# Second scale and shift on transposed columns, modulation units summed in groups, and a new order from the first norm to the first expert

## The chip, the cores and the metric

The kernel runs on one core of a Trainium2 chip. The metric is the device time in microseconds (us) of one launch; a smaller time is better. The engines are PE (TensorE), DVE (VectorE), ACT (ScalarE), POOL (GpSimd) and SP (SyncE, which here only issues DMAs). Each takes its own instructions in the order of the program; semaphores order them against each other.

## What is computed

One layer on 384 tokens (128 context tokens and 256 latent ones), three tiles of 128 tokens, D = 1024 features. The reference, cut to what matters:

```
sh1, sc1, g1, sh2, sc2, g2 = silu(cond) @ w_ada + b_ada      # for two conditions: context, latent
h  = x * (1 + sc1) + sh1
u  = h @ w_in                                                # 1536 columns
mix = concat(rglru(conv(u_r)) * gelu(u_g), fourier(u_f)) @ w_out
x  = layer_norm(ALPHA * x + g1 * mix, ln1_g, ln1_b)
h2 = x * (1 + sc2) + sh2
y2 = hier_moe(h2)      # logits; best of 4 groups; best 2 of its 4 experts; 16 SwiGLU experts
x  = layer_norm(ALPHA * x + g2 * y2, ln2_g, ln2_b)
```

## The kernel before

Weights stream through a ring of SBUF slots, one unit of 2 MB (1024 x 512 floats) a slot. The first 17 units (`p1_units`) are twelve of w_ada, three of w_in and two of w_out; six slots hold them. Then come 48 units of the experts (gate, up, down of 16 experts), with a seventh slot. SP issues each load when its slot is free: it waits for `p1_used` in the first part and for `unit_used` in the experts, both of which PE raises when it has consumed a unit. The seventh slot lies over `rows` and is free when POOL has finished the first norm (`x1_done`).

**Modulation.** For each w_ada unit, `ada_sums` runs 8 matmuls of 32 x 512 into a PSUM bank (two of the 32 rows are in use, one a condition), ACT copies the bank to `mrow` (`ada_rows`), PE turns it into columns of `modT` by 4 tiny matmuls (`ada_cols`), and DVE adds the bias (`mod_out`). In the middle of the kernel these units (4 to 9) stand in a row between the Fourier work and the output projection.

**Output projection, norm, h2.** PE computes `mix` for tile 0, 1, 2 in two halves of 512 columns each (L1447, 8 matmuls a half; what the text calls the mix). Between the quarters it makes six rows by L1431 (g1, 1+sc2 and sh2, for both conditions, each copied to all partitions), which ACT copies to SBUF. DVE multiplies by the g1 row, adds ALPHA * x, takes the statistics, and applies scale and shift in token-major form with the sc2 and sh2 rows (`tts`). PE transposes `tts` (L1460), ACT copies it to `h2T`, and PE computes the router logits (L1466). ACT rounds `tts` to `h2H`, DVE takes the rest `h2L`; the pair feeds the dispatch.

**Routing.** DVE picks group and experts from the logits with a chain of small operations (L927 to L965), PE turns the marks into ranks (L1490, L1495; called rank below), DVE builds the selection matrices `sel` (`pick` L984, `pick2` L994, six of each), the counts `cnt` (`route_done`), `io` and the weights `comb`. The **dispatch** (L1509) multiplies h2H and h2L by `sel`: 16 blocks n, 6 matmuls each, in the four PSUM banks 4 to 7; from n = 4 on it waits until ACT has copied block n-4 out (`x_out`, L577). ACT then copies the columns of one expert to `xs` (`x_in`), and PE starts the first expert (L1553).

**Experts.** `project_in(e, 0)`, `project_in(e, 1)`, `turn`, `project_out`, `combine` for e = 0 to 15, software pipelined; then the second norm on DVE.

The order on every engine is written by hand. In the text, start of the picks means the first L984.

Of the kernel before, what the change touches and what calls it, by code (L numbers as in the profile page):

```python
# [15 lines left out]
P = 128  # L16
D = 1024
# [41 lines left out]
C_ROW = C_SUM + 2  # L59
# [17 lines left out]
def constants():  # L77
# [10 lines left out]
    for q in range(2):  # L88
        c[q::32, C_SUM + q] = 1
# [24 lines left out]
def build(nc, t):  # L114

    ctx = ExitStack()
    with ctx:
# [15 lines left out]
        def keep(name, shape, dt=F32):  # L133
# [13 lines left out]
        cond32 = keep("cond32", [P, KD, 32])  # L147
# [24 lines left out]
        tts3 = at("tts3", A0 + 6144, [P, NT, D])  # L172
        tts = [tts3[:, i, :] for i in range(NT)]
# [48 lines left out]
        rows = at("rows", rows0, [P, 8, D])  # L222
# [22 lines left out]
            "x1_done h2_done mod2_done h2hi h2lo h2T_ps h2T_sb lg_ps assign_done rank_ps route_done "  # L245
# [47 lines left out]
        ADA_GROUPS = [2, 4, 6, 10, 12]  # L293
        ADA_UNIT = [0, 1, 3, 4, 7, 8, 9, 10, 11, 12, 15, 16]
        ADA_COUNT = [1, 2, 3, 4, 8, 9, 10, 11, 12, 13, 16, 17]

        ABANK = [6, 6, 4, 6] + [6, 4] * 3 + [6, 6]
# [4 lines left out]
        ]  # L302

# [54 lines left out]
        def _(sp):  # L358
# [54 lines left out]
        def _(act):  # L413
# [28 lines left out]
            def ada_rows(n):  # L442

                act.wait_ge(s["p1_used"], ADA_COUNT[n])
                need(act, "modT_ps", n)
                act.copy(mrow[:, :], PS[:, ABANK[n], :]).then_inc(s["mrow_sb"], 1)  # L446

# [82 lines left out]
            for n in range(4, 10):  # L530
                ada_rows(n)


            act.wait_ge(s["yr_done"], CR)
            for r in range(6):
                act.wait_ge(s["row_ps"], r + 1)
                act.copy(rows[:, r, :], PS[:, 6:8, :].rearrange("p a n -> p (a n)")).then_inc(s["row_sb"], 1)
                if r == 1:
                    root(NT)
                if r == 0:  # L540
                    for k, n in enumerate(("ln1_g", "ln1_b")):
                        act.dma_start(rows[:, 6 + k, :], t[n].partition_broadcast(P)).then_inc(s["ln1_in"], 16)


            def h2_copies(i):
                act.wait_ge(s["h2T_ps"], i + 1)
                act.copy(h2T[:, :, i * P:(i + 1) * P], PS[:, 2 * i:2 * i + 2, :].rearrange("p a (k n) -> p (a k) n", n=P))\
                    .then_inc(s["h2T_sb"], 1)

            def h2_high(i):  # L550
                act.wait_ge(s["h2_done"], i + 1)
                if i == 0:
                    act.wait_ge(s["p1_used"], 15)
                act.copy(h2H[:, i, :], tts[i]).then_inc(s["h2hi"], 1)

            root(NT + 1)
            ada_rows(10)
            h2_high(0)
            h2_copies(0)
            root(NT + 2)  # L560
            ada_rows(11)
            h2_high(1)
            h2_copies(1)
            h2_copies(2)
            h2_high(2)

            act.wait_ge(s["assign_done"], 1)
# [11 lines left out]
            act.wait_ge(s["route_done"], 1)  # L579
            for n in range(KD):  # L580
                if n == 0:
                    act.wait_ge(s["h2lo"], NT)
                    act.wait_ge(s["lg_ps"], 1)
                x_out(n)
            act.wait_ge(s["prow_ps"], 1)
            act.copy(Prow[:, :, :], PS[:, 2:4, 0:TOK]).then_inc(s["prow_sb"], 1)
            for n in range(KD, 2 * KD):
                x_out(n)


            counts = {}

            def x_in(e):
# [4 lines left out]
                if e == 0:  # L598
# [3 lines left out]
                if e >= 2:  # L602
                    used(act, unit(e - 2, 1))
# [44 lines left out]
            x_in(0)  # L648
# [46 lines left out]
        def _(dve):  # L695
# [41 lines left out]
            dve.tensor_copy(cond32[:, :, 0:2], cond[:, :, :]).then_inc(s["cond_done"], 1)  # L737
# [29 lines left out]
            def mod_out(n):  # L767

                c0 = ADA[n][0] * KD + 4 * ADA[n][1]

                dve.wait_ge(s["modT_ps"], next(g for g in ADA_GROUPS if g > n))
                dve.tensor_tensor(modT[:, c0:c0 + 4, :], PS[:, 7, 2 * c0:2 * c0 + 8].rearrange("p (n s) -> p n s", s=2),
                                  cols[:, A_BADA + c0:A_BADA + c0 + 4].unsqueeze(2).broadcast_to([P, 4, 2]),
                                  ALU.add).then_inc(s["mod_sb"], 1)

            def modulate(hf):

                mod_out(2 * hf)
                mod_out(2 * hf + 1)
                dve.wait_ge(s["mod_sb"], 2 * hf + 2)  # L780
# [89 lines left out]
            for n in range(4, 10):  # L870
                mod_out(n)
            dve.wait_ge(s["mod_sb"], 10)


            sc2 = modT[:, SC2 * KD:SC2 * KD + KD, :]
            sh2 = modT[:, SH2 * KD:SH2 * KD + KD, :]
            g1col = cols[:, A_L1G:A_L1G + KD].unsqueeze(2).broadcast_to([P, KD, 2])
# [857 lines left out]
```

## Time and profile before

| | |
|---|---|
| device time, 3 runs | 543.44 us median (543.39 to 551.8) |
| the profiled execution | 546.24 us |
| its span, first to last instruction | 544.4 us |
| PE, DVE, ACT, POOL busy | 465.0, 244.5, 120.6, 61.4 us |
| mean granted clock of PE | 0.936 |
| moved by DMA | 146.64 MB |

The profiled execution took 546.24 us, of which 544.4 are between its first and its last instruction. Positions below are us from the start of this span. A granted clock of 1.00 is 2.4 GHz, one of 0.50 is 1.2 GHz; a value between is a stretch in which both occurred. An fp32 matmul stands in the trace as two records, so the 8 matmuls of `ada_sums` are "x16" and 8 transposes may be "x8" or more.

### The profile page before, as it was taken

What the parts mean: (1) busy time and instruction counts of PE and PEld (TensorE: products, weight loads), DVE (VectorE), ACT (ScalarE), POOL (GpSimd) and SP (SyncE); (2) the same over time, 40 slices, a digit from 0 to 9 for tenths busy, and PEclk for the clock granted to TensorE, in tenths of its full rate; (3) what the DMA queues carried; (4) which work ended last, traced back from release to release, by engine and by line L of the source; (5) the groups of instructions that cost most, each with busy time, mean ns of one, the idle gap of its engine ahead of it and who ended that gap; (6) DMA issues with size and microseconds to landing.
All of it is one profiled execution on the core that took longest, in us unless ns stands there. A gap on an engine that the chain in (4) does not pass through costs nothing.

```text
span 544.4 us, 6675 instructions
## 1 busy us (share of the span) xinstructions
PE 465.0 (85%) x2488; PEld 261.0 (48%) x2488; DVE 244.5 (45%) x440; ACT 120.6 (22%) x224; POOL 61.4 (11%) x59
## 2 busy tenths in 40 slices
PE   0788997979899999839799999999999999899600
PEld 0444554647455653739645545455555554454200
DVE  2552626580314319565011324444444444334797
ACT  2300177841210220313401111111111111021100
POOL 1000042673400006610000000000000000000000
PEclk9989999998999999858999999999999999999855
DMA  8999692200999405950059999999999999999002
GB/s 321 387 386 291 244 390 68 96 1 18 308 389 387 169 1 184 391 198 2 1 195 389 390 392 340 396 395 393 391 393 394 395 395 393 392 391 377 11 2 116
DMA packets 64868, 146.64 MB, mean 269 GB/s; under 512 B 3560, under 2 KB 4392, under 8 KB 64824
## 3 DMA queue, kind: packets, MB, share of 16 engines
q1 hardware_dynamic: 63776, 143.66, 71.4%
q10 hardware_dynamic: 888, 2.28, 1.1%
q8 instruction: 30, 0.49, 0.4%
q0 software_dynamic: 160, 0.10, 0.3%
q14 instruction: 14, 0.11, 0.1%
HBM read 144.45 MB, written 1.58 MB: 268 GB/s over the span
## 4 chain that ended last, share of the span: by engine, by line
PE 73%; DVE 12%; DMA 5%; issue 5%; ACT 4%; ACTq 0%; SPq 0%; DVEq 0%
PE PS L1547 16%; PE PS L1346 9%; PE PS L1585 8%; PE PS L1447 8%; PE PS L1553 5%; PE PS L1284 4%; PE PS L1620 4%; DMA ring<-in_ex_w_gate 4%; PE PS L1509 4%; PE PS L1431 2%; PE PS L1295 2%; PE PS L1329 2%; PE PS L1466 2%; PE PS L1592 1%; PE PS L1627 1%
## 5 line engine op out<-in xcount | busy, mean ns | idle before, releaser
L1547 PE MATMUL PS<-ring,xs 128*64 128x256 f32 x896 | 103.1, 382 | 1.8 <-DMA ring<-in_ex_w_gate 1.1
L1547 PEld LDWEIGHTS PS<-ring,xs 128*64 128x64 f32 x896 | 62.4, 137 | 37.9 <-issue 9.7
L1346 PE MATMUL PS<-hT,ring 128*128 128x388 f32 x192 | 68.3, 510 | 3.8 <-DVE hT L793 3.8
L1585 PE MATMUL PS<-ring,hTs 128*64 128x512 f32 x224 | 52.7, 613 | 1.3 <-DMA ring<-in_ex_w_down 0.8
L1098 DVE SCALAR_TENSOR_TENSOR y<-PS,comb,y 128x1024 f32<-128x1024 f32 x42 | 53.5, 1277 | 0.3 <-PE PS L1627 0.3
L1346 PEld LDWEIGHTS PS<-hT,ring 128*128 128x128 f32 x192 | 37.8, 198 | 31.4 <-issue 5.2
L1553 PE MATMUL PS<-ring,xs 128*128 128x512 f32 x64 | 28.1, 594 | 2.9 <-ACT xs L611 2.9
L1585 PEld LDWEIGHTS PS<-ring,hTs 128*64 128x64 f32 x224 | 15.2, 140 | 31.4 <-issue 31.3
L645 ACT CAST yh<-PS 128x512 fp32r<-128x512 f32 x14 | 8.2, 586 | 97.9 <-PE PS L1585 58.1
L1084 DVE TENSOR_TENSOR yl<-PS,yh 128x512 fp32r<-128x512 f32 x14 | 9.7, 692 | 43.9 <-ACT yh L645 43.9
L1620 PE MATMUL PS<-yh,selT 64*128 64x512 f32 x84 | 21.0, 496 | 4.6 <-DVE y L1098 2.6
L1284 PE MATMUL PS<-ring,cond 128*32 128x512 f32 x192 | 23.4, 611 | 0.0
L1447 PE MATMUL PS<-ring,yfs 128*128 128x512 f32 x48 | 23.4, 633 | 0.0
L1054 DVE SCALAR_TENSOR_TENSOR hid<-sg,PS 128x256 f32<-128x256 f32 x14 | 5.9, 422 | 38.7 <-PE PS L1547 38.7
L1447 PE MATMUL PS<-ring,mixT 128*128 128x512 f32 x48 | 21.6, 592 | 0.0
L1620 PEld LDWEIGHTS PS<-yh,selT 64*128 64x128 f32 x84 | 8.0, 186 | 26.2 <-issue 26.1
L1553 PEld LDWEIGHTS PS<-ring,xs 128*128 128x128 f32 x64 | 12.0, 190 | 17.2 <-issue 17.1
L1509 PE MATMUL PS<-sel,h2H 128*128 128x384 f32 x48 | 17.9, 373 | 2.6 <-DVE sel L994 2.6
L1219 POOL TENSOR_SCALAR gtmp<-gtmp 128x388 f32<-128x388 f32 x8 | 9.5, 1188 | 85.9 <-ACT gtmp L481 85.9
L1295 PEld LDWEIGHTS PS<-cst,mrow 128*128 128x128 f32 x96 | 11.7, 191 | 13.1 <-ACT mrow L446 7.3
L446 ACT COPY mrow<-PS 128x512 f32<-128x512 f32 x12 | 7.0, 586 | 46.8 <-PE PS L1284 37.9
L1509 PE MATMUL PS<-sel,h2L 128*128 128x384 f32 x48 | 17.3, 360 | 0.0
(230 smaller groups left out, 601.3 us busy)
## 6 DMA issues: line engine op xcount, KB each, us to landing
ring<-in_ex_w_gate SPq DMA_DIRECT2D x16, 2048.0 KB, 13.8
ring<-in_ex_w_up SPq DMA_DIRECT2D x16, 2048.0 KB, 14.0
ring<-in_ex_w_down SPq DMA_DIRECT2D x16, 2048.0 KB, 14.5
ring<-in_w_ada SPq DMA_DIRECT2D x12, 2048.0 KB, 14.8
ring<-in_w_in SPq DMA_DIRECT2D x3, 2048.0 KB, 20.6
ring<-in_w_out SPq DMA_DIRECT2D x2, 2048.0 KB, 12.4
xn<-in_x_sample SPq DMA_DIRECT2D x2, 512.0 KB, 6.5
pos<-in_pos SPq DMA_DIRECT2D x2, 512.0 KB, 7.5
```

What stands on the lines that cost most here:

```text
L1098: dve.scalar_tensor_tensor(out=y12[:, i, :], in0=src, scalar=comb[:, i, e:e + 1], in1=y12[:, i, :], op0=ALU.mult, op1=ALU.add).then_inc(s[ ...
L1284: mm = pe.matmul(PS[32 * j:32 * j + 32, ABANK[n], :], cond32[:, k, :], w[:, k, :], start=(k < 4), stop=(k >= 4))
L1295: mm = pe.matmul(PS[:, 7, 2 * (c0 + q):2 * (c0 + q) + 2], mrow[:, q * P:(q + 1) * P], cst[:, C_SUM:C_SUM + 2], start=True, stop=True)
L1329: mm = pe.matmul(PS[:, 4 + gi, 0:W], wbd[:, 8 * gi + 4 * d + c, :], xc[:, c, :], start=True, stop=True)
L1346: mm = pe.matmul(PS[:, w % 4, 0:W], wt[:, k, (w % 4) * P:(w % 4 + 1) * P], hT[:, k, :], start=(k == 0), stop=(k == KD - 1))
L1431: mm = pe.matmul(PS[:, 6 + k // 4, (k % 4) * P:(k % 4 + 1) * P], modT[:, j * KD + k, q:q + 1].broadcast_to([P, P]), ident, start=True, sto ...
L1447: mm = pe.matmul(PS[:, 2 * i + h, :], x, unit3(ring[(14 + h) % RING])[:, c, :], start=(n == 0), stop=(n == KD - 1))
L1509: mm = pe.matmul(PS[:, 4 + n % 4, 0:HS], part[:, i, k * P:(k + 1) * P], sel[:, i, h * HS:(h + 1) * HS], start=(i == 0 and part is h2H), st ...
L1547: mm = pe.matmul(PS[HALF * h:HALF * (h + 1), j, 0:FE // 2], x[:, k, 0:HALF], w[:, k, h * (FE // 2):(h + 1) * (FE // 2)], start=(k == 0), s ...
L1553: mm = pe.matmul(PS[:, j, :], x[:, k, :], w[:, k, :], start=(k == 0), stop=(k == KD - 1))
L1585: mm = pe.matmul(PS[HALF * h:HALF * (h + 1), 3, :], x, w[:, f, h * 512:(h + 1) * 512], start=(f == 0), stop=(f == KF - 1))
L1620: mm = pe.matmul(PS[:, b + h, :], m[HALF * h:HALF * (h + 1), i * P:(i + 1) * P], part[HALF * h:HALF * (h + 1), 0:512], start=(q == 0), sto ...
```

## The change

- **Modulation in groups.** The twelve units form five groups (0-1, 2-3, 4-5, 6-9, 10-11). The window of `cond32` is shifted by two columns a member, so all members add up in one PSUM bank in different rows; one `ada_rows`, one `ada_cols` and one `mod_out` serve a group. The g1 group gets no columns: `g1_row` makes both g1 rows directly from `mrow` with two 512-column matmuls a condition, and DVE adds the bias row `bg1` (a new 0.5 MB DMA).
- **Second scale and shift feature-major.** DVE only normalises (`x1n`); PE transposes the normalised x (`x1_cols`), and ACT applies scale and shift while it copies to `h2T` (DVE for half of tile 2). The token-major h2 for the dispatch is made by transposing h2T back (`back`, 3 x 8 transposes). The four sc2 and sh2 rows are gone. ln1_g and ln1_b of tile 2 are applied feature-major too (`x1_feat`, 8 more transposes); POOL does tiles 0 and 1.
- **Norm by halves.** DVE's norm work starts after half a tile's mix; tile 2 is normalised in two halves.
- **Order.** The last two w_ada units (10 and 11) move behind the third logits; the routing finds the best two in all groups at once; the weights of the experts' outputs (`gap_done`, two exps on ACT, `comb`) move behind the picks; `pick`/`pick2` alternate strictly; the pw rows (L1523 before, L1573 now) move ahead of the dispatch; the first four dispatch blocks run tile by tile; the first expert reads `xTa` and `xTb` without the copy to `xs`; the seventh slot is loaded as the third expert unit.

The core of the diff:

```diff
-            for v, e, j in order:
+            for v, e, j in [order[0], order[1], order[RING]] + order[2:RING] + order[SLOTS:]:
...
-                    sp.wait_ge(s["x1_done"], NT)
+                    sp.wait_ge(s["yf_ps"], FG)
+                    sp.wait_ge(s["yr_done"], CR)
+                    sp.wait_ge(s["tri_done"], 1)
...
             x_cols(1)
-            ada_rows(0)
             root(2)
             x_cols(2)
-            for n in range(1, 4):
-                ada_rows(n)
+            ada_rows(GA)
+            ada_rows(GB)
...
+            act.wait_ge(s["state_done"], 8)
+            act.dma_start(bg1[:, :], ...).then_inc(s["bg1_in"], 16)
+            ada_rows(GG1)
             act.wait_ge(s["yr_done"], CR)
-            for r in range(6):
-                act.wait_ge(s["row_ps"], r + 1)
-                act.copy(rows[:, r, :], PS[:, 6:8, :].rearrange("p a n -> p (a n)")).then_inc(s["row_sb"], 1)
...
+            act.wait_ge(s["gap_done"], 1)
             act.activation(rt[:, 6, :, 0:NG], rt[:, 5, :, 0:NG], ACT.Exp).then_inc(s["pos_pool"], 1)
             act.activation(rs[:, 5, :], rs[:, 4, :], ACT.Exp).then_inc(s["pos_pool"], 1)
...
+            act.wait_ge(s["x1n"], NT + 1)
+            act.wait_ge(s["prow_ps"], 1)
+            act.copy(Prow[:, :, :], PS[:, 0:2, 0:TOK]).then_inc(s["prow_sb"], 1)
+            for n in range(2 * KD):
+                if n == KD // 2:
+                    act.wait_ge(s["x1_done"], NT)
+                x_out(n)
...
+            for m in range(2 * NT):
+                if m == 2:
+                    low_part(2)
+                pick(m)
+                pick2(m)
...
+            step(dve.tensor_tensor(rt[:, 5, :, 0:NG], gl, wide(rs[:, 0, :], NG), ALU.subtract))
+            link(dve.tensor_tensor(rt[:, 4, :, 0:NG], mx2, mx1, ALU.subtract))
+            link(dve.tensor_tensor(rt[:, 4, :, 0:NG], rt[:, 4, :, 0:NG], og, ALU.mult))
+            link(dve.tensor_reduce(rs[:, 4, :], rt[:, 4, :, 0:NG], AX.X, ALU.add))
+            dve.nop().then_inc(s["gap_done"], 1)
             dve.wait_ge(s["pos_pool"], 2)
...
             def h2_high(i):
-                act.wait_ge(s["h2_done"], i + 1)
...
+                act.wait_ge(s["h2b_ps"], i + 1)
+                act.copy(h2H[:, i, :], token_ps(i)).then_inc(s["h2hi"], 1)
```

The first place is on PE, from the last half of the mix to the rank matmuls. Names: `ring` with `cond` is a w_ada unit, `mrow` its columns, `wr` with `h2T` the logits, `tts` the token-major h2, `marks` the rank. Before:

```order
L1447 MATMUL PS<-ring_52,mixT 128x512 x4
L1284 MATMUL PS<-ring_53,cond_64 32x512 [waits mrow_sb,ring_in4,row_sb]
L1295 MATMUL PS<-cst,mrow 128x2 [waits mrow_sb,mod_sb]
L1460 MATMUL PS<-cst,tts_84 128x128 [waits h2_done]
L1284 MATMUL PS<-ring_54,cond_64 32x512 [waits mrow_sb,ring_in5]
L1295 MATMUL PS<-cst,mrow 128x2 [waits mrow_sb]
L1460 MATMUL PS<-cst,tts_84 128x128 [waits h2_done]
L1466 MATMUL PS<-wr,h2T 128x20 [waits h2T_sb,rtr_in]
L1466 MATMUL PS<-wr,h2T 128x20 [waits h2T_sb]
L1460 MATMUL PS<-cst,tts_84 128x128 [waits h2_done]
L1466 MATMUL PS<-wr,h2T 128x20 [waits h2T_sb]
L1490 MATMUL PS<-marks_58,tri_ones 128x16 [waits assign_done,tri_done]
```

The same place now (L1512 logits, L1519 back, L1485 `x1_cols`, L1537 the transposes of tile 2's x, L1334 a w_ada unit):

```order
L1499 MATMUL PS<-ring_52,mixT 128x512 x4
L1512 MATMUL PS<-wr,h2T 128x20 [waits h2T_sb,rtr_in]
L1519 MATMUL PS<-cst,h2T 128x128 [waits h2T_sb]
L1512 MATMUL PS<-wr,h2T 128x20 [waits h2T_sb]
L1519 MATMUL PS<-cst,h2T 128x128 [waits mrow_sb,mod_sb]
L1485 MATMUL PS<-cst,xn 128x128 [waits x1n]
L1512 MATMUL PS<-wr,h2T 128x20 [waits ev_dve,h2T_sb]
L1519 MATMUL PS<-cst,h2T 128x128 [waits h2lo]
L1334 MATMUL PS<-ring_53,cond_64 32x512 [waits h2T_sb,ring_in4]
L1537 MATMUL PS<-cst,tmp_85 128x128 [waits x1T_sb]
L1334 MATMUL PS<-ring_54,cond_64 32x512 [waits h2T_sb,ring_in5]
L1544 MATMUL PS<-marks_58,tri_ones 128x16 [waits assign_done,tri_done]
```

The logits of tiles 0 and 1 come straight behind the mix, and both w_ada units and 8 transposes now stand between the last logits and the rank.

The second place is on ACT, the two exps and the copies out of the dispatch. Before:

```order
L554 CAST h2H<-tts_84 128x1024 [waits h2_done]
L568 ACT_TABLE_LOAD
L568 ACTIVATE rt<-rt 128x3x4 [waits assign_done]
L569 ACTIVATE rs<-rs 128x3
L577 COPY xTa<-PS 128x384 [waits lg_ps,disp_ps,h2lo,route_done]
L577 COPY xTa<-PS 128x384 [waits disp_ps] x3
```

Now:

```order
L592 COPY xn<-PS 128x1024 [waits x1b_ps]
L595 ACT_TABLE_LOAD
L595 ACTIVATE rt<-rt 128x3x4 [waits gap_done]
L596 ACTIVATE rs<-rs 128x3
L608 COPY Prow<-PS 128x768 [waits prow_ps,x1n]
L604 COPY xTa<-PS 128x384 [waits disp_ps] x4
```

The exps keep their place ahead of all copies out of the dispatch, while what they wait for, `gap_done`, is now raised on DVE behind all picks, the counts and `io`.

The third place is DVE between the rank and `gap_done`. Now (L959 `low_part(2)`, L1025 `pick`, L1032 `pick2`; four more pairs, the counts, twelve `io` operations and four for `gap_done` follow):

```order
L1017 TENSOR_REDUCE pw<-rt 128x3
L1025 TENSOR_SCALAR selA<-cst,pw 128x384 [waits dve_step,h2b_ps,iota_in]
L1032 SCALAR_TENSOR_TENSOR sel<-cst,pw,selA 128x384 [waits selA_done]
L1025 TENSOR_SCALAR selA<-cst,pw 128x384
L1032 SCALAR_TENSOR_TENSOR sel<-cst,pw,selA 128x384 [waits selA_done]
L959 TENSOR_TENSOR h2L<-PS,h2H 128x1024 [waits h2hi]
```

Before, the first `pick2` stood behind the second `pick`, and the third h2L part stood ahead of the rank's results:

```order
L896 TENSOR_TENSOR h2L<-tts_84,h2H 128x1024 [waits h2_done,h2hi]
L971 TENSOR_TENSOR rt<-PS,rt 128x48 [waits rank_ps]
L984 TENSOR_SCALAR selA<-cst,pw 128x384 [waits dve_step,iota_in]
L984 TENSOR_SCALAR selA<-cst,pw 128x384
L994 SCALAR_TENSOR_TENSOR sel<-cst,pw,selA 128x384 [waits h2T_ps,h2lo,selA_done]
```

So one 1024-wide operation moved into the picks, and every `pick2` now waits for the `pick` just ahead of it.

## Rows read from the trace of the kernel before

**Rows 1.** The page's 40 equal slices: granted clock in tenths, and GB/s moved.

```profile
PEclk9989999998999999858999999999999999999855
...
GB/s 321 387 386 291 244 390 68 96 1 18 308 389 387 169 1 184 391 198 2 1 195 389 390 392 340 396 395 393 391 393 394 395 395 393 392 391 377 11 2 116
```

**Rows 2.** Windows: stretch, PE, PEld, DVE, ACT, POOL busy (records), PEclk, DMA share, GB/s.

```profile
380.00:420.00 40.00, 40.00 (x288) 19.98 (x286) 18.28 (x24) 6.53 (x16) 0.00 (x0) 1.00 1.04 393
```

**Rows 3.** Timeline of SP: start, us, what it issues.

```profile
221.34 0.37 SPq L387 DMA_DIRECT2D ring<-in_ex_w_gate  x1
...
230.63 0.37 SPq L387 DMA_DIRECT2D ring<-in_ex_w_up  x1
...
275.83 0.37 SPq L387 DMA_DIRECT2D ring<-in_ex_w_down  x1
```

**Rows 4.** Timeline of the start: start, us, engine, line, operation [idle before, releaser].

```profile
22.64 0.59 ACT L446 COPY mrow<-PS 128x512 f32<-128x512 f32 x1 [1.87 <-PE PS L1284]
...
24.43 1.09 PE L1307 MATMUL PS<-cst,xn 128*128 128x128 f32 x8
...
31.07 7.14 PE L1346 MATMUL PS<-hT,ring 128*128 128x388 f32 x16 [1.94 <-DVE hT L793]
```

**Rows 5.** Timeline of PE from the middle w_ada units to the mix.

```profile
141.39 1.92 PE L1284 MATMUL PS<-ring,cond 128*32 128x512 f32 x16
...
158.26 1.05 PE L1295 MATMUL PS<-cst,mrow 128*128 128x2 f32 x8
...
160.96 5.38 PE L1447 MATMUL PS<-ring,yfs 128*128 128x512 f32 x8
...
169.60 3.60 PE L1447 MATMUL PS<-ring,yfs 128*128 128x512 f32 x8
...
173.04 1.95 PE L1431 MATMUL PS<-cst,modT 128*128 128x128 f32 x16
```

**Rows 6.** The issue of the first w_out unit, at 143.4, to its landing.

```profile
DMA to landing us min/median/max: 12.1/12.1/12.1
```

**Rows 7.** A window of 3 us, columns as in Rows 2.

```profile
225.00:228.00 3.00, 3.00 (x21) 3.00 (x21) 0.97 (x1) 0.02 (x1) 3.00 (x1) 0.68 1.02 401
```

**Rows 8.** Timeline from the end of the mix to the routing.

```profile
214.75 1.93 PE L1284 MATMUL PS<-ring,cond 128*32 128x512 f32 x16
...
223.81 4.79 PE L1466 MATMUL PS<-wr,h2T 128*128 128x20 f32 x32
...
228.42 1.95 PE L1460 MATMUL PS<-cst,tts 128*128 128x128 f32 x8
...
231.47 3.61 PE L1466 MATMUL PS<-wr,h2T 128*128 128x20 f32 x16 [1.10 <-ACT h2T L547]
...
235.11 0.22 DVE L927 TENSOR_TENSOR lg<-PS,rb 128x60 f32<-128x60 f32 x1 [9.14 <-PE PS L1466]
...
241.12 0.21 DVE L965 TENSOR_TENSOR before<-rt 128x48 bf16<-128x48 f32 x1
```

**Rows 9.** Timeline from the picks to the first expert.

```profile
243.19 0.95 DVE L984 TENSOR_SCALAR selA<-cst,pw 128x384 f32<-128x384 f32 x2
...
244.06 0.61 DVE L994 SCALAR_TENSOR_TENSOR sel<-cst,pw,selA 128x384 fp32r<-128x384 f32 x1
...
249.06 0.16 DVE L1007 TENSOR_REDUCE small<-totoff 128x1 f32<-128x16 f32 x1
...
249.81 0.86 ACT L577 COPY xTa<-PS 128x384 f32<-128x384 f32 x2 [8.55 <-DVEq L1014]
...
252.27 0.17 DVE L1022 TENSOR_SCALAR io<-io 128x16 f32<-128x16 f32 x1
...
268.68 13.99 PE L1553 MATMUL PS<-ring,xs 128*128 128x512 f32 x32 [2.92 <-ACT xs L611]
```

**Rows 10.** The chain that ended last, the dispatch in two halves: start, us.

```profile
244.81 11.27 PE PS L1509 x48
...
257.42 8.35 PE PS L1509 x48
```

More of the change, by code:

```diff
@@ L58 @@
 C_SUM = C_COD4 + 4
[L59 removed]
+C_ROW = C_SUM + 8
 C_SEG = C_ROW + 4
@@ L87, in constants @@
     c[:, C_SEG:C_SEG + 3 * NE] = (np.arange(3 * NE) % NE != 0)
-    for q in range(2):
+    for q in range(8):
         c[q::32, C_SUM + q] = 1
@@ L170, in build @@
         A0 = place[0]
-        tts3 = at("tts3", A0 + 6144, [P, NT, D])
-        tts = [tts3[:, i, :] for i in range(NT)]
+        bg1 = at("bg1", A0 + 6144, [P, D])
+        tmp2 = at("tmp2", A0 + 10240, [P, 2, D])
         h2T = at("h2T", A0 + 18432, [P, KD, TOK])
@@ new lines, in _, with h2_cols @@
+            for k, n in enumerate(("ln1_g", "ln1_b")):
+                act.dma_start(rows[:, 2 + k, :], t[n].partition_broadcast(P)).then_inc(s["ln1_in"], 16)
+            ada_rows(GD)
+            def h2_cols(i, ks):
+                q = 1 if i else 0
+                for k in ks:
+                    if k % 4 == 0:
+                        act.wait_ge(s["xh_ps"], 2 * i + k // 4 + 1)
+                    last = act.activation(h2T[:, k, i * P:(i + 1) * P], PS[:, 2 * i + k // 4, (k % 4) * P:(k % 4 + 1) * P],
+                                          ACT.Identity, bias=modT[:, SH2 * KD + k, q:q + 1],
+                                          scale=modT[:, SC2 * KD + k, q:q + 1])
+                last.then_inc(s["h2T_sb"], 1)
@@ new lines, in token_ps, with x1_feat @@
+            def token_ps(i):
+                return PS[:, BACK[i]:BACK[i] + 2, :].rearrange("p a n -> p (a n)")
+            def h2_high(i):
+                act.wait_ge(s["h2b_ps"], i + 1)
+                act.copy(h2H[:, i, :], token_ps(i)).then_inc(s["h2hi"], 1)
+            x1T = tmp2[:, 1, :].rearrange("p (k n) -> p k n", n=P)
+            def x1_feat(hf):
+                if hf:
+                    act.wait_ge(s["ev_dve"], 1)
+                for k in range(4 * hf, 4 * hf + 4):
+                    last = act.activation(x1T[:, k, :], PS[:, 4 + hf, (k % 4) * P:(k % 4 + 1) * P], ACT.Identity,
+                                          bias=cols[:, A_L1B + k:A_L1B + k + 1], scale=cols[:, A_L1G + k:A_L1G + k + 1])
+                last.then_inc(s["x1T_sb"], 1)
@@ L919, in _ @@
-            for n in range(10, 12):
-                mod_out(n)
+                dve.tensor_tensor(h2L[:, i, :], PS[:, BACK[i]:BACK[i] + 2, :].rearrange("p a n -> p (a n)"),
+                                  h2H[:, i, :].bitcast(F32), ALU.subtract).then_inc(s["h2lo"], 1)
             low_part(0)
-            low_part(1)
             dve.wait_ge(s["lg_ps"], 1)
@@ L1504, in dispatch @@
                     pe.wait_ge(s["disp_sb"], n - 3)
-                for i in range(NT):
+                for i in tiles:
                     if k == 0:
                         pe.wait_ge(s["sel_done"], h * NT + i + 1)
+                        pe.wait_ge(s["h2lo"], i + 1)
                     for part in (h2H, h2L):
```

462 lines of the change are left out of this document (245 added, 217 removed).

## The prediction

> **What bounds the kernel now.** I read the slices first. From slice 20 on (about 275 us) the DMA moves 390 GB/s or more without a break until the last weights are in, while slices 17 to 19 move almost nothing [rows 1]. So the expert stage is a stream of weights, but the stream does not start by itself: SP issues the seventh and last free slot at 230.63 and nothing more until 275.83, when the first expert's first unit has been consumed [rows 3]. From there 41 of the 48 units and the two ln2 rows are still to come: 41 x 2.10 MB + 1.05 MB = 87 MB, at 393 GB/s [rows 2] 221 us, which fills the time to 497; the last expert's work and the second norm follow. PE is busy all of that stage too [rows 2]. Nothing in it is anchored to the launch. Whatever brings the start of the first expert (268.68, [rows 9]) forward moves the first free slot, the stream and the end by the same amount, and the change leaves everything behind that point as it was. The question is only how far 268.68 moves, and it hangs on one chain of PE, DVE and ACT, which I follow in five stretches.
>
> **A. The start.** Today ACT takes the square root of the third tile behind a copy to `mrow`, which starts at 22.64 when PE has consumed the first w_ada unit, and PE's third transposes start at 24.43 [rows 4]. In the change the copy is gone from there; the transposes can start when PE is free, near 22.7, so the second unit comes some 1.7 us earlier. Behind it one group of columns instead of two shortens the next gap too: four tiny matmuls, about 1.0 us as in [rows 5], leave PE ahead of the second half of h. That is 1.7 + 0.8 = **2.5 us** for all that follows up to the middle w_ada units. If the second unit's landing holds PE, only the 0.8 stay; its 7.0 MB, with all ahead of it, are through at some 20 us by the first two slices [rows 1], so I keep 2.5.
>
> **B. The middle w_ada units.** From 141.39 to the mix at 160.96 are 19.5 us [rows 5]. Six blocks of columns at 1.0 (5.9 without overlap) and waits of about 0.8 for `mrow` leave; two `g1_row` come, 4 matmuls of 512 columns, each 0.86 us by the mix (16 records of 0.43 a half tile; eight take 3.44 and show as 3.60 in [rows 5]), so 3.4. New length 16.3 us: the mix could start at 155.2. A first unit of w_out must have landed. It is issued when the first of these units is consumed and takes 12.1 us [rows 6], so from 140.8 to 152.9; the new `bg1` row (0.5 MB, 1.3 us at 390 GB/s) is ahead of it in time, and the ln1 rows (1.05 MB, 2.7 us) are now issued while it runs. That gives 152.9 to 156.9. I take the mix at 155.8, a gain of **5.2 us** so far; the ends are 5.8 and 4.1. What the trace shows here is a unit that needs 12.1 us while its own bytes need 5.4; it is sharing. The Trainium skill (DMA: Bandwidth & Descriptors, Issuing engines are not separate DMA queues) says that DMAs of all issuing engines run on the same 16 engines and interleave. By that rule the ln1 rows take their share from w_out and the start lies near 156.9; with a queue of its own for ACT it would be 155.2.
>
> **C. The mix.** Six half tiles of 8 matmuls at 0.86 are 41.3 us and stay. Today six blocks of 16 records at 1.78 (1.95 in [rows 5], with overlap) stand between them, 10.7 us, and the first four matmuls take 5.38 instead of 3.60, since the clock is low after the pauses of the columns: 53.8 us in all, to 214.75 [rows 8]. Now there are one block of columns (1.0) and two of 8 transposes (0.93 each, half of the 1.95 that [rows 8] shows at the low clock): 44.1 us if the clock holds, since PE comes out of 16 us of matmuls without the pauses. The mix ends at **199.9**, 14.9 us earlier. DVE is not late: it has two bias rows and six more 1024-wide operations to do after the second `g1_row` at about 151.5, and the first half tile ends at 162.7 (estimate, 8 x 1.3 us). If the clock falls as today, 1.8 us are lost.
>
> **D. From the end of the mix to the picks.** Today this takes 28.4 us (214.75 to 243.19, [rows 8, 9]). In the change all is on PE, in order; DVE's statistics of the last half, some 4 us, hide under it, so the halves of tile 2 themselves bring nothing. At the end of such a stretch today the clock falls: PE is busy 3.00 of 3 us with logits and transposes, and the granted clock is 0.68, then 0.50 [rows 7]; 16 records of logits then take 3.61 instead of half of that, 8 transposes 1.95 [rows 8]. A share of 0.68 in that window puts the fall at 226, some 4.7 us after the last w_ada unit was consumed (221.34, [rows 3]). I take the same: logits 1.8 and transposes 0.9 at 2.4 GHz, then logits 2.8, transposes 1.8 and 1.8; 4 small DVE operations (1.1, between 4 x 0.17 and 4 x 0.43, the `io` and copy rows of [rows 9]); logits 3.6: logits complete after 13.9. Then transposes 1.8, a w_ada unit 3.5, transposes 1.4, a unit 1.9 (with the clock back in the second half, as it came back 5 us into the dispatch): 22.5. DVE's choice needs 6.0 us today (235.11 to 241.12) and about 5.0 with five operations fewer at 0.24, so it is ready at 18.9 and **waits 3.6 us for PE**, behind the two w_ada units and the transposes. From there to the first pick 1.8, as today: 24.3. Gain **4.1 us**. With the clock up throughout the same steps take 17.2, with it down throughout 26.5.
>
> **E. From the picks to the first expert.** Today 25.5 us (243.19 to 268.68). The change makes this longer. `gap_done` stands on DVE behind the six pairs of picks, now 0.48 + 0.61 each since every second one waits for the first (6.5 us; today all of it is 5.9, 243.19 to 249.06), behind `low_part(2)` (1.25), behind counts and `io` (3.3, to 252.27 and its end), and 4 operations more (0.9): 12.0 us after the first pick. On ACT the two exps wait for it, and behind them are queued the copy of Prow and all sixteen `x_out`. PE fills its four banks and then needs the first copy. So the fifth block starts after 12.0 + 0.3 (exps) + 0.8 (Prow) + 0.5 (copy) = 13.6 us, PE idle for the last 4 of them. Twelve blocks follow, 6 x 0.174 = 1.04 each by 48 matmuls in 8.35 [rows 10]: 12.5. The clock will be low when they start, which cost 11.27 - 8.35 = 2.9 today [rows 10]; I take 2.3. The g2 columns and the states' transpose, now inside, 1.3; the last copy 0.8 (0.35 + 0.48). Sum 30.5: **5.0 us lost**, of which the dropped copy to `xs` has already given back 2.1 (2.92 of waiting becomes 0.8, [rows 9]). Here the row shows a copy that stood 8.55 us behind a wait for DVE [rows 9], harmless today since the banks filled only then. The Trainium skill (TensorE: Matmul & The Clock Gate, Architectural detail: the array is 16x 32x32, not 1x 128x128) states that ScalarE's queue is strictly first in, first out. By it the stall is certain; if copies could pass the exps, the fifth block would start some 4 us earlier.
>
> **Other edits.** The seventh slot is loaded some 50 us before 230.63, and the units behind it land by 226; none is needed before 254. At most it costs nothing. POOL's two tiles end by 199 and no longer overlap DVE's second tile. `st_row` and the g2 bias (under 3 us of DVE) are done before the last block. The first expert reads its columns from `xTa`: 32 weight loads, 0.19 each, hidden under matmuls of 0.43. Each is taken at 0; the uncertainty of all together is 1 us either way.
>
> **Sum.** 14.9 + 4.1 - 5.0 = 14.0 us. The first expert starts at 254.7, the first slot is free near 262, the span is 530.4 and the profiled execution 532.2 against 546.24. The profiled one lies 2.8 above the median of the runs, so the forecast for the median is 543.44 - 14.0 = **529.4 us**, 2.6% faster.
>
> **Rivals.**
> *The clock stays up* from the mix to the dispatch: D gives 11.2 instead of 4.1, E loses 4; 14.9 + 11.2 - 4.0 = 22, so 521. For it: PE works without the pauses for `mrow`. Against: it fell today with PE busy [rows 7]. Chance 0.15.
> *Less is gained*: w_out late (1.1), a low clock at the mix (1.8), the low clock through D (2.2), 1 us of E: gain 8, so 535.5. Chance 0.2. Here also falls the case that the change does not do what it says, since the halves and the shorter choice hide behind PE's own queue.
> *The gain stops at the stream.* If the weights were bound to the launch and not to the first free slot, 0 would be left: 543. Against it stands the empty stretch from 230.63 to 275.83 [rows 3]. Chance 0.03.
> *Slower.* The stall in E lets the clock fall to 1.2 GHz and it does not come back until the first expert is through: twelve blocks cost 25 instead of 12.5 + 2.3, the two units of expert 0 28 instead of 14 us [rows 9], together 24 against the 14 gained: 553.6. It decides against the change once the clock stays low for 28 us of dense work. Today the dispatch's first half lost only 2.9 us to it, so it came back some 5 us after 244.81 [rows 10]: 0.02.
> The forecast itself (gain 10 to 18) has 0.6.
>
> **Numbers.** Faster by over 2% (under 532.6; about what a measurement of this kernel can tell from no change) takes all of the first rival and nearly all of the forecast: 0.73. Within 2%: 0.24. Slower 0.03. The range from 520.5 to 537 holds the first two rivals and the forecast.
>
> **What would show it.** In the profile after: the mix starting near 156 and ending near 200; logits, then w_ada units and transposes ahead of the rank, DVE waiting for it; ACT's exps waiting for DVE with x_out behind, and PE idle some 4 us after the fourth block; the first expert near 255; SP's first expert issue after the pause near 262; the same 269 us from there to the end. I am wrong if the clock does not fall in D, if PE waits elsewhere (for ACT's small activations, or w_out), or if the stream loses its pace.

## The result and the profile after

The changed kernel took 526.53 us (median of 4 runs, 524.57 to 532.98) where the kernel before took 545.98 (4 runs, 543.39 to 551.8). The ratio is 0.9647 with a 95% interval of 0.9545 to 0.9749. The forecast was 529.4. The profiled execution is the longest of the four, 532.98 us with a span of 530.9, 13.3 us below that of before (546.24); the sum gave 532.2 for it. It is a slow one, at a mean granted clock of 0.938 where the other three have 0.950 to 0.956, so what hangs on the clock in it is read beside a second profile below.

The slices of the page, as in [rows 1] (slices of 13.3 us):

```profile
PEclk9979999998999997798999999999999999999855
...
GB/s 318 387 386 303 319 367 83 77 0 22 325 389 387 367 86 243 103 215 2 56 341 397 394 364 365 394 394 395 394 391 391 394 395 395 394 392 344 1 1 119
```

The hole in the transfers is still there (slices 18 and 19, counted from 0) and the even stream behind it still starts at slice 20, now of a shorter span. The weights follow the first expert, as the prediction said. SP's first issue behind the pause, the counterpart of 275.83 in [rows 3], comes 14.06 us earlier:

```profile
223.35 0.37 SPq L393 DMA_DIRECT2D ring<-in_ex_w_gate  x1
261.77 0.37 SPq L393 DMA_DIRECT2D ring<-in_ex_w_down  x1
```

The timeline of PE, from the end of the middle w_ada units to the rank (start, us, line, operation, idle before and releaser), answers to [rows 5, 8]:

```profile
137.96 1.92 PE L1334 MATMUL PS<-ring,cond 128*32 128x512 f32 x16
...
150.89 3.64 PE L1334 MATMUL PS<-ring,cond 128*32 128x512 f32 x32
156.52 5.40 PE L1499 MATMUL PS<-ring,yfs 128*128 128x512 f32 x8 [1.99 <-DMA ring<-in_w_out]
...
202.16 1.86 PE L1512 MATMUL PS<-wr,h2T 128*128 128x20 f32 x16
...
212.42 3.58 PE L1512 MATMUL PS<-wr,h2T 128*128 128x20 f32 x16 [1.55 <-DVE h2T L952]
...
217.70 2.71 PE L1334 MATMUL PS<-ring,cond 128*32 128x512 f32 x16
```

The chain that ended last has that unit's load as a piece of its own (start, us):

```profile
139.94 16.53 DMA ring<-in_w_out
```

The mix starts at 156.52 instead of 160.96, having waited 2.0 us for the w_out unit, and is over at 202.16 instead of 214.75. From there to the first expert, on DVE, ACT and PE, against [rows 9, 10]:

```profile
220.97 0.21 DVE L1006 TENSOR_TENSOR before<-rt 128x48 bf16<-128x48 f32 x1
...
223.94 0.21 DVE L1012 TENSOR_TENSOR rt<-PS,rt 128x48 f32<-128x48 f32 x1 [1.63 <-PE PS L1544]
224.83 0.82 DVE L1025 TENSOR_SCALAR selA<-cst,pw 128x384 f32<-128x384 f32 x1 [0.22 <-DVE pw L1017]
...
236.30 0.21 ACT L595 ACTIVATE rt<-rt 128x12 f32<-128x12 f32 x1 [10.14 <-DVEq L1067]
236.42 0.19 ACT L596 ACTIVATE rs<-rs 128x3 f32<-128x3 f32 x1
236.51 0.78 ACT L608 COPY Prow<-PS 128x768 f32<-128x768 f32 x1
237.19 1.63 ACT L604 COPY xTa<-PS 128x384 f32<-128x384 f32 x4
```

```profile
237.72 0.69 PE L1563 MATMUL PS<-sel,h2H 128*128 128x384 f32 x1 [6.61 <-ACT xTa L604]
...
254.61 3.69 PE L1624 MATMUL PS<-ring,xTa 128*128 128x512 f32 x8 [0.70 <-ACT xTb L604]
```

ACT stands 10.14 us in front of the first exp, waiting for `gap_done`; the copies out of the dispatch are queued behind it, and PE has nothing to do for 6.61 us ahead of the fifth block.

The control, a second profile of the same kernel (529.62 us, span 527.5), has the same order with other clock stretches. Its third logits, the end of DVE's wait for the rank, its first pick, fifth block and first expert:

```profile
202.92 1.86 PE L1512 MATMUL PS<-wr,h2T 128*128 128x20 f32 x16
...
210.73 2.74 PE L1512 MATMUL PS<-wr,h2T 128*128 128x20 f32 x16 [1.55 <-DVE h2T L952]
...
222.25 0.21 DVE L1012 TENSOR_TENSOR rt<-PS,rt 128x48 f32<-128x48 f32 x1 [2.47 <-PE PS L1544]
223.14 0.82 DVE L1025 TENSOR_SCALAR selA<-cst,pw 128x384 f32<-128x384 f32 x1 [0.22 <-DVE pw L1017]
...
236.03 0.69 PE L1563 MATMUL PS<-sel,h2H 128*128 128x384 f32 x1 [6.60 <-ACT xTa L604]
...
251.73 3.69 PE L1624 MATMUL PS<-ring,xTa 128*128 128x512 f32 x8 [0.70 <-ACT xTb L604]
```

The five stretches in us; the measured ones are differences of two starts in the traces, the last row the rest of the span:

| stretch | before | predicted | first profile | control |
|---|---|---|---|---|
| A, to the first middle w_ada unit | 141.39 | 138.9 | 137.96 | 141.15 |
| B, to the mix | 19.57 | 16.9 | 18.56 | 17.82 |
| C, the mix | 53.79 | 44.1 | 45.64 | 43.95 |
| D, to the first pick | 28.44 | 24.3 | 22.67 | 20.22 |
| E, to the first expert | 25.49 | 30.5 | 29.78 | 28.59 |
| first expert starts | 268.68 | 254.7 | 254.61 | 251.73 |
| from there to the end | 275.7 | 275.7 | 276.3 | 275.8 |

### The profile page after: what moved, and what is told of

Its sections match the earlier page's. It is cut to its first block, busy times and chain, and to the rows that moved or that the text cites. A ratio compares the mean times of both kernels' runs of the same rounds, so it can differ in the third digit from the quotient of the medians.

```text
span 530.9 us, 6436 instructions
## 1 busy us (share of the span) xinstructions
PE 455.0 (86%) x2368; PEld 248.2 (47%) x2368; DVE 240.1 (45%) x439; ACT 117.1 (22%) x235; POOL 53.9 (10%) x57
## 4 chain that ended last, share of the span: by engine, by line
PE 72%; DVE 13%; DMA 8%; ACT 3%; issue 3%; ACTq 0%; DVEq 0%; SPq 0%
PE PS L1618 17%; PE PS L1401 9%; PE PS L1656 8%; PE PS L1499 8%; PE PS L1624 5%; PE PS L1691 4%; DMA ring<-in_ex_w_gate 4%; DMA ring<-in_w_out 3%; PE PS L1563 3%; PE PS L1334 3%; PE PS L1663 3%; PE PS L1384 2%; PE PS L1512 1%; PE PS L1698 1%; DMA rowB<-in_colsB 1%
## 5 line engine op out<-in xcount | busy, mean ns | idle before, releaser
L1334 PE MATMUL PS<-ring,cond 128*32 128x512 f32 x192 | 24.3, 629 | 0.0
L1691 PEld LDWEIGHTS PS<-yh,selT 64*128 64x128 f32 x84 | 7.8, 183 | 26.4 <-issue 26.3
L1090 DVE SCALAR_TENSOR_TENSOR sg<-sg,PS 128x256 f32<-128x256 f32 x14 | 5.9, 422 | 25.1 <-ACT sg L645 25.1
L1691 PE MATMUL PS<-yl,selT 64*128 64x512 f32 x84 | 16.8, 396 | 0.0
L936 DVE TENSOR_TENSOR tmp<-PS,rows 128x512 f32<-128x512 f32 x6 | 4.2, 692 | 27.5 <-PE PS L1499 27.5
L645 ACT ACTIVATE sg<-PS 128x256 f32<-128x256 f32 x14 | 5.4, 384 | 49.6 <-PE PS L1618 49.6
## 6 DMA issues: line engine op xcount, KB each, us to landing
ring<-in_ex_w_gate SPq DMA_DIRECT2D x16, 2048.0 KB, 13.8
ring<-in_w_out SPq DMA_DIRECT2D x2, 2048.0 KB, 17.9
```

The source lines that it names most:

```text
L1334: mm = pe.matmul(PS[32 * j:32 * j + 32, SUM_BANK[g], :], cond32[:, k, 6 - 2 * m:38 - 2 * m], w[:, k, :], start=(m == 0 and k < 4), stop=(l ...
L1691: mm = pe.matmul(PS[:, b + h, :], m[HALF * h:HALF * (h + 1), i * P:(i + 1) * P], part[HALF * h:HALF * (h + 1), 0:512], start=(q == 0), sto ...
```

## The experiments

Each kernel was timed in five rounds beside the kernel before, in three groups of four; 545.3, 545.5 and 549.0 us were the medians of the kernel before beside them. The intervals of the ratios are 0.005 to 0.008 wide to either side, 3 to 5 us, and a difference of two such ratios is uncertain by 4 to 5 us. By the timing alone only the exps, the three edits together and the row blocks are told apart from the control, and the operand alone from the kernel before; what the other runs say is read from one trace each. Differences are against the control's 527.76 us unless another is named; the last four runs had a kernel before of 549.0 us beside them and are compared by their ratios, with the control's 0.9673.

**Control.** The changed kernel again. 

> The changed kernel unchanged, as the control of the runs beside it. Expected 18 to 20 us less than the kernel before in the timed runs if the extra gain over the predicted 14.0 is real, 14 us if it was chance. In its trace the first expert starts 14 us earlier than in the kernel before (near 254.6); if it starts at 249 or 250 with the same sequence of instructions, the surplus over 14.0 is the clock in stretches B to E of one execution and not another mechanism.

Measured: 527.76 us median (526.32 to 530.71), ratio 0.9673 (0.9625 to 0.9721), so 17.8 us less than before; one profile to the other 16.9 (544.4 to 527.5). The first expert starts at 251.73, 3.0 before the forecast: D and E are 4.1 and 1.9 shorter than forecast, A and B 2.3 and 0.9 longer. The surplus in D is clock. Windows of 3 us over it (stretch, PE busy, PEclk, DMA share, GB/s), first the first profile, then the control:

```profile
204.00:207.00 3.00, 3.00 (x25) 0.78 0.86 302
207.00:210.00 3.00, 3.00 (x15) 0.50 0.96 356
...
216.00:219.00 3.00, 3.00 (x16) 0.50 0.00 0
219.00:222.00 3.00, 3.00 (x28) 0.94 0.10 10
```

```profile
207.00:210.00 3.00, 2.18 (x20) 1.00 1.03 395
210.00:213.00 3.00, 2.27 (x15) 0.78 0.14 51
213.00:216.00 3.00, 3.00 (x15) 0.50 0.00 0
216.00:219.00 3.00, 3.00 (x19) 0.59 0.00 0
219.00:222.00 3.00, 3.00 (x42) 1.00 0.58 187
```

Neither keeps the clock up through D; the control loses it later and for about half as long.

**The exps behind the eighth copy.**

```diff
-            act.wait_ge(s["gap_done"], 1)
-            act.activation(rt[:, 6, :, 0:NG], rt[:, 5, :, 0:NG], ACT.Exp).then_inc(s["pos_pool"], 1)
-            act.activation(rs[:, 5, :], rs[:, 4, :], ACT.Exp).then_inc(s["pos_pool"], 1)
...
             for n in range(2 * KD):
...
                 x_out(n)
+                if n == 7:
+                    act.wait_ge(s["gap_done"], 1)
+                    act.activation(rt[:, 6, :, 0:NG], rt[:, 5, :, 0:NG], ACT.Exp).then_inc(s["pos_pool"], 1)
+                    act.activation(rs[:, 5, :], rs[:, 4, :], ACT.Exp).then_inc(s["pos_pool"], 1)
```

> The wait for gap_done and the two exps go behind the eighth copy out of the dispatch on ACT; nothing else moves. Theory (stretch E): the copy of Prow and the first x_out no longer stand behind DVE, so PE's 6.6 us ahead of the fifth block go, of which part comes back as a wait for the sel of the second half (ready some 11 us after the first pick) ahead of the ninth block or for the exps; first expert 4 to 6 us earlier, time 4 to 6 us less than the changed kernel. Rival 1: the idle time only moves to the ninth block, since the selection of the second half and tile 2 is as late: 0 to 1 us. Rival 2: without the pause the clock does not fall either, and the two low stretches of the dispatch go too: 7 us less.

Measured: 519.62 us (515.0 to 523.11), ratio 0.9491 (0.9425 to 0.9558), 8.1 less by the medians and 9.9 by the ratios (0.0182 of 545.3). ACT's copies start as soon as PE has blocks:

```profile
221.82 0.80 ACT L605 COPY Prow<-PS 128x768 f32<-128x768 f32 x1 [1.56 <-PE PS L1574]
225.51 1.63 ACT L601 COPY xTa<-PS 128x384 f32<-128x384 f32 x4 [2.89 <-PE PS L1564]
...
232.50 0.21 ACT L612 ACTIVATE rt<-rt 128x12 f32<-128x12 f32 x1
```

```profile
240.62 3.69 PE L1625 MATMUL PS<-ring,xTa 128*128 128x512 f32 x8 [0.70 <-ACT xTb L601]
```

From the first pick to the first expert are 20.4 us (220.23 to 240.62) instead of the control's 28.6, and the clock is 1.00 all through 222 to 258. This is the second rival of the expectation: the pause costs its own 6.6 and what the clock loses behind it (1.3 in the control, by the next run). Nothing waits at the ninth block.

**The pause filled.** Two lines ahead of the fifth block:

```diff
+            for _ in range(7):
+                pe.matmul(PS[:, 2, :], ident, mrow[:, :], start=True, stop=True)
```

> Seven 128x512 matmuls whose result is not used stand on PE behind the first four dispatch blocks, inside its pause ahead of the fifth; the wait itself stays. They need 6.0 us at 2.4 GHz. If what the pause costs beyond its own 6.6 us is the low clock behind it (0.50 from 237 to 243 in the changed kernel), the fifth to tenth blocks run at 1.04 us instead of 1.7 and the first expert starts 2.5 us earlier. Rival: the clock falls in the dispatch whether PE pauses or not (it fell in the kernel before with PE busy); then 0, or up to 1 us more where the added matmuls outlast the pause.

Measured: 526.14 us, ratio 0.9660 (0.9603 to 0.9716), 1.6 less, which the timing cannot tell from nothing.

```profile
226.60 6.17 PE L1582 MATMUL PS<-mrow,cst 128*128 128x512 f32 x14
233.36 0.44 PE L1563 MATMUL PS<-sel,h2H 128*128 128x384 f32 x1 [0.58 <-ACT xTa L604]
```

From the fifth block to the first expert are 14.4 us (233.36 to 247.73), against 15.7 in the control (236.03 to 251.73) and 16.9 in the first profile (237.72 to 254.61). So the low clock behind the pause costs 1.3 to 2.5 us, and it is the pause that brings it: with PE kept busy the windows from 231 to 249 show 1.00. The twelve profiles of the changed kernel and its variants agree: the nine that have the pause show 0.50 behind it, and the three without it (this run, the exps behind the eighth copy, all three edits) show 1.00 through the dispatch.

**The ln1 rows later.** `ada_rows(GD)` ahead of the two ln1 DMAs instead of behind. 

> The two ln1 rows (1.05 MB) are issued by ACT behind the copy of the fourth modulation group instead of ahead of it, so after the first w_out unit has landed. Theory (stretch B): they took their share of the DMA engines from that unit; it lands 2 to 3 us earlier (near 153.9 where 156.5 was measured) and the mix starts 2.0 us earlier, when PE is ready (154.5): 2.0 us less, 3.8 if the low clock at the mix's start goes too. Rival: the unit is late because of the bg1 row and the other weight units behind it; then the mix starts at 156.5 as before and nothing changes. POOL needs the ln1 rows near 185, so their own delay costs nothing by either.

Measured: 527.23 us, ratio 0.9668 (0.9616 to 0.9721), 0.5 less. In the trace PE goes into the mix without a wait, and the two w_out units take 14.9 us from issue to landing (median), against 17.9 and 17.5 in the first profile and the control:

```profile
150.23 3.64 PE L1334 MATMUL PS<-ring,cond 128*32 128x512 f32 x32
153.80 3.70 PE L1499 MATMUL PS<-ring,yfs 128*128 128x512 f32 x8
```

That fits the theory, but it isn't proof: of the ten profiles with the rows in their early place, eight show a wait here, of 0.8 to 2.4 us, and two show none. The median from issue to landing is 15.3 to 18.3 us in the ten, and 14.9 and 14.2 in the two profiles with the rows late (this one and that of all three edits). The waits of the ten are 1.2 us on average, which is what the edit can bring; the timing cannot see that.

**The rank first.** `ada_sums(11)` behind the rank matmuls. 

> The rank matmuls stand ahead of the last w_ada unit on PE instead of behind it. Theory (stretch D): DVE's marks are ready 2.5 us (1.6 in the first profile of the changed kernel) before PE reaches the rank, and everything up to the copies out of the dispatch hangs on DVE's chain from there, so picks, gap_done and the fifth block come 1.8 us earlier and the first expert with them: 1.8 us less. Rival: PE needs the unit's columns (mrow) for the pw rows and is then late itself; the dispatch starts 0.5 us earlier at most, but the fifth block still follows DVE, so by this rival the gain is between 0 and 0.5 only if PE and not DVE sets the fifth block.

Measured: 524.62 us, ratio 0.9610 (0.9555 to 0.9665), 3.1 less. From the end of the third logits to the first pick are 8.0 us (213.16 to 221.14) against 9.7 in the control (213.47 to 223.14); PE's pause ahead of the fifth block shrinks from 6.60 to 5.24:

```profile
220.25 0.21 DVE L1012 TENSOR_TENSOR rt<-PS,rt 128x48 f32<-128x48 f32 x1 [0.78 <-PE PS L1543]
```

```profile
233.88 0.69 PE L1563 MATMUL PS<-sel,h2H 128*128 128x384 f32 x1 [5.24 <-ACT xTa L604]
```

The fifth block comes 20.7 us behind the third logits, 22.6 in the control: the 1.8 of the theory. In this profile 1.2 of it is lost again behind the fifth block (16.9 from there to the first expert, 15.7 in the control), where the clock is low for longer.

**All three.** 

> Three edits together: exps behind the eighth copy out of the dispatch, ln1 rows behind the fourth group, rank ahead of the last w_ada unit. If they add, 8 (the exps, as timed) + 1.5 (ln1, as in its trace) + 0.5 (rank: with the stall gone the dispatch follows PE's pw rows, not DVE's gap_done, so most of its 1.8 is hidden) = 10 us less than the changed kernel, 517.5. Rival: the rank still gives 1.8, so 11.5 less. Rival: w_out's earlier landing gives nothing in the timed runs, as when it was alone, so 8.5 less.

Measured: 515.23 us (514.3 to 520.57), ratio 0.9468 (0.9404 to 0.9532): 12.5 less than the changed kernel. It is the shortest median of all, but the timing does not tell it from the exps alone (0.9491). Its profile (515.32 us) starts the first expert at 236.93. Against the kernel with the exps alone, the picks come 1.7 us sooner behind the third logits (7.1 against 8.8), and 1.0 of that is given back between picks and first expert (21.4 against 20.4), since PE's pw rows are then the later ones. The rank's own share with the stall gone is 0.65 us, as expected. The first expert is 3.7 us earlier than with the exps alone; of the rest 1.7 lie in B, where PE does not wait for w_out, and 1.75 in D up to the third logits, where the clock is low for a shorter time in this profile, while A gives 0.4 back.

**The row blocks back in the mix.**

```diff
+                    for _ in range({(0, 0): 0, (2, 1): 2}.get((i, h), 1)):
+                        for k in range(KD):
+                            pe.matmul(PS[:, 2 * i + h, 0:P], modT[:, k, 0:1].broadcast_to([P, P]), ident, start=True, stop=True)
```

> Six blocks of eight 128x128 matmuls, whose results are overwritten and not used, stand again inside the mix, as many as the rows of the kernel before had there (one ahead of each half tile but the first, two ahead of the last). Theory (stretch C): PE is the only bound there, so the mix gets 6 x 1.78 = 10.7 us longer and the whole kernel 10.7 us slower; this is the largest term of the sum. Rival: DVE's norm or w_out sets the pace in part and the blocks hide; then the mix's end moves less than 8. Rival: the extra work only shifts where the clock falls, 9 to 13.

Measured: 538.20 us, ratio 0.9883 (0.9821 to 0.9945), 10.4 more. The mix lasts 54.67 us (154.33 to 209.00) against 43.95 in the control: 10.72 more for six blocks, 1.79 each.

```profile
170.85 1.95 PE L1497 MATMUL PS<-cst,modT 128*128 128x128 f32 x16
172.63 3.60 PE L1502 MATMUL PS<-ring,yfs 128*128 128x512 f32 x8
```

Start to start, such a block is 1.78 us, with nothing hidden.

**The copy to xs back.** `x_in(0)` ahead of `x_in(1)`, and PE reads `xs` for expert 0. 

> The first expert gets its columns through the copy to xs again, as in the kernel before; nothing else changes. Theory (stretch E): PE waits 2.9 us again where it now waits 0.7 to 0.8, so 2.1 us slower. Rival: the copy is hidden behind PE's own queue, 0. Rival: more, since the pause lets the clock fall under the first expert's matmuls: 2.1 plus up to 5.

Measured: 531.26 us, ratio 0.9723 (0.9666 to 0.9779), 3.5 more.

```profile
252.44 15.52 PE L1619 MATMUL PS<-ring,xs 128*128 128x512 f32 x32 [2.92 <-ACT xs L636]
```

The wait is 2.92 as in [rows 9], 2.2 more than 0.70. The two units then take 15.52 us instead of 13.99, at a granted clock of 0.52 in the window from 252 to 255. In this profile the copy costs 2.2 and the low clock 1.5. That the wait brought the low clock is not shown: in the kernel before the same wait of 2.92 us stands ahead of the same matmuls [rows 9], the granted clock is 1.00 from 262 to 283, and they take 13.99.

**The operand alone, in the kernel before.** The reverse of that edit. 

> The kernel before with one edit: the first expert reads its columns from xTa and xTb, without the copy to xs. Theory (stretch E): its wait of 2.92 us becomes 0.7, nothing else moves, so 2.2 us less than the kernel before. Rival, from the run that put the copy back into the changed kernel (3.7 slower, half of it by a low clock under the first expert): more than 2.2 where the clock would have fallen, up to 3.7. Rival: 0, hidden behind the first slot's load.

Measured: 543.91 us median of 12 beside 548.99 of before, ratio 0.9931 (0.9884 to 0.9978): 3.8 us less, between 1.2 and 6.4. In its trace PE waits 0.70 and the picks are 23.0 us ahead of the first expert (242.59 to 265.56) instead of 25.5. The operand gives 2.2 to 2.5 in the trace; the interval is too wide to say that it gives more.

**The seventh slot late.** The old order and the old wait on `x1_done`. 

> The seventh slot is loaded again behind the first norm and in its old place in SP's queue; the rest is the changed kernel. Theory: it lands some 20 us ahead of its use, so the time is the same (within 0.5 us). Rival: SP's queue stands behind x1_done, the units behind it are issued later and share the DMA engines with each other, and the first expert or the second waits for one: 1 to 5 us slower.

Measured: 526.56 us, ratio 0.9645 (0.9582 to 0.9708). The seventh unit is issued at 218.99 and SP's next one at 254.74, behind a first expert at 247.58; from there to the end are 275.6 us. Nothing in the trace waits for it, and the timing shows no difference.

**The last norm whole.** 

> Tile 2 is normalised in one operation of 1024 columns instead of two of 512. Theory (stretch D): PE's transposes of tile 2 stand behind logits and transposes of tiles 0 and 1, 5.2 us after the mix, and the normalised tile is there by then, so nothing changes (within 0.3 us). Rival: the second half is late for its transposes and all behind it follows: 0.6 us slower.

Measured: 530.52 us, ratio 0.9661 (0.9577 to 0.9745), no difference by the ratio. The third logits start 7.82 us behind the mix (202.90 to 210.72), in the control 7.81. The halves bring nothing in the traces.

**A copy at the start.**

```diff
+            act.wait_ge(s["p1_used"], 1)
+            act.copy(mrow[:, :], xn[:, 0, 0:512])
             root(2)
```

> A copy of 512 columns to mrow, whose result is not used, stands again on ACT between the first w_ada unit and the square root of the third tile, where the kernel before had its first modulation copy; the later copies stay. Theory (stretch A): PE's third transposes start 0.8 to 1.0 us later and everything behind them with it, so 0.8 to 1.0 us slower, where the prediction gave this copy 1.7. Rival: the second w_ada unit or DVE's h hides it, 0. Rival: 1.7 as predicted.

Measured: 531.09 us, ratio 0.9722 (0.9655 to 0.9788), 2.7 more by the ratio. The expectation was too low, and the prediction's 1.7 nearly right:

```profile
25.69 1.09 PE L1366 MATMUL PS<-cst,xn 128*128 128x128 f32 x8 [1.90 <-DVE xn L772]
26.71 3.39 PE L1336 MATMUL PS<-ring,cond 128*32 128x512 f32 x16
```

PE waits 1.90 us where it doesn't wait in the control, and the second unit then takes 3.39 instead of 1.92 at the low clock. The second part of the projection starts at 53.75, in the control at 50.26: 3.5 us, mostly the 1.9 of waiting and 1.5 of clock. But at the first middle w_ada unit only 0.2 is left (141.39 against 141.15): on the way two groups took 2.93 and 3.40 us at the low clock in the control where they take 1.54 and 1.89 here. So the trace prices the wait, not the end of A.

## Why the prediction was right

The frame holds. Fourteen profiles have between 274 and 278 us from the first expert to the end, wherever that expert starts. A gain ahead of it arrives whole, and the row blocks show it in the timing too (10.7 in the mix, 10.4 in the medians and 11.5 by the ratios). The slices of [rows 1] were misread by one place: slice 17 still moves 198 GB/s, and only 18 and 19 are nearly empty; the argument needs no more. The rival in which the stream stops the gain is out, and so is the slower one: the clock behind the stall came back some 5.5 us after the fifth block's start, not after 28 (0.50 in the windows from 237 to 243, 0.96 in the next).

That the first profile's 254.61 meets 254.7 is in part luck: against the forecast A, D and E came out 0.9, 1.6 and 0.7 us shorter, B and C 1.7 and 1.5 longer.

**A** (2.5 predicted). The run with the copy puts its wait at 1.9. The second saving is 0.8 as forecast: from the w_ada unit after the first half of h to the next one are 8.05 us before (38.15 to 46.20) and 7.26 in both profiles after. That makes 2.7. The first profile shows 3.4 and the control 0.2, since the clock fell at other places on the way; the eleven profiles of the changed kernel and its variants without the copy have the first middle w_ada unit between 137.3 and 141.5. In the control one gate matmul group took 2.93 us where the first profile has 1.54, for instance. The step was right in its mechanism; a spread of 4 us by the clock was not in its bounds.

**B** (2.7). 1.0 and 1.75 measured. PE's own work came out as summed, near 16.5. The w_out unit was later than the value taken, at 156.5, near the upper end of 156.9 that went by shared engines. The row bears that side out: 16.53 us from issue to landing in the chain, where [rows 6] has 12.1 and the upper end allowed 16.1. This is the term of B that was too small. The Trainium skill (DMA: Bandwidth & Descriptors, Issuing engines are not separate DMA queues) has DMAs of all issuers interleave; the run with the late ln1 rows agrees with it but doesn't settle it.

**C** (9.7, the largest term). 8.15 and 9.84 measured. "If the clock holds" was true in the control (43.95, against 44.1) and false in the first profile, whose first four matmuls took 5.40 as in [rows 5]; in nine of the eleven profiles without the row blocks the mix takes 43.94 or 43.95. The six blocks cost 10.72 by the run that puts them back, against 10.7.

**D** (4.1). 5.8 and 8.2 measured: the term that was sized worst. Nine profiles have D's instructions as the changed kernel has them; they take 18.6 to 22.7 us, 20.0 on average, and the forecast of 24.3 lies above all of them. The order of waits is the one forecast: DVE done at 221.2 and waiting 1.63 us for PE behind both w_ada units, where 3.6 were forecast (2.47 in the control). Up to the third logits the first profile agrees (13.8 us after the mix, forecast 13.9); behind them the first w_ada unit took 2.71 and not 3.5. The control needs 10.6 up to that point. The step took one profile's low clock as a constant, and the low stretch is what varies between executions. Its two ends were also summed wrongly: by its own terms D is 16.6 us with the clock up throughout and 29.7 with it down throughout, not 17.2 and 26.5 (26.3 is what a low clock behind the third logits alone gives). The halves of tile 2 bring nothing, as said.

**E** (5.0 lost). 4.3 and 3.1 lost. `gap_done` came 11.4 us after the first pick (12.0 forecast). The stall itself was 6.6 us instead of 4, because the first four blocks ran at the full clock and were done sooner; the fifth block came 12.9 us after the first pick, 13.6 forecast. What stood behind was sized at 2.3 for the clock (1.3 and 2.5 measured) and 2.1 for the operand (2.2). That ACT's copies cannot pass the exps is shown by the run that moves the exps: 8.1 us.

**From the sum to the median.** The sum gave 14.0 from profile to profile and 13.3 came out in the first pair, 16.6 in the second. The timed runs say 17.8 to 19.3. Most of the surplus is D: with the 20.0 us that its nine profiles have on average, in place of 24.3, the sum gives 18.3 (an estimate). The kernel before has 28.4 and 28.8 there in the two profiles that leave D alone, so the gain is on the changed side. The mean granted clocks agree with it: 0.937 to 0.956 in ten executions of the changed kernel, 0.947 on average, and 0.928 to 0.943 in 39 of the kernel before, 0.937 on average. The sum had this only as the rival of 0.15 in its extreme form, which none of the profiles shows. The profiled execution was also taken to lie 2.8 above the median, and it lies 6.5 above it.

## What to carry to other kernels

Find the one event from which the rest of the kernel runs at a fixed length, show it by the empty stretch ahead of it, and then account only for what lies before it. When a wait is moved on an engine that takes its instructions in order, price everything that is queued behind it: here two tiny exps ahead of sixteen copies cost 8 of the 26 us that the change would have brought. A pause of PE can cost more than its own length: the 6.6 us here brought 1.3 to 2.5 us of low clock behind it. Take a term that hangs on the clock from several profiles, not from one; the single low stretch taken for D was 4 us too long.

## What the runs showed of the hardware

- The clock fell in the first profile while PE was busy all the time, with narrow work: the window from 204 to 207 shows 3.00 of 3 us busy and 0.78, and those from 207 to 219, with 128x20 logits, 128x128 transposes and a 32-row unit, show 0.50, most of them with 3.00 of 3 us busy. In the mix, with 128-row matmuls of 512 columns, it was 1.00 from 162 on. Two other profiles show such a fall; in the control the clock falls only behind PE's wait of 1.55 us ahead of the third logits, so the runs do not say that narrow work alone brings it.
- Waits ahead of wide matmuls do not always show in the clock: behind 2.92 us it was 0.52 for 3 us in the run with the copy to `xs` and 1.00 in the kernel before, at the same place; behind 0.70 in the control it was 1.00.
- The same program gives profiles that stand 3 us apart at the end of A with waits equal within 0.2 us: only matmul durations differ (15.91 and 17.60 us for the same 48 records of the projection).
- The table load of the exps took 1.28 us; between copies of the dispatch PE did not wait for it.
